# Gate and up projections in ten of eleven steps as seven block products instead of eight

## The reference

```python
D_FF = 2816
h2 = rms_norm_2(x, g_ffn[layer])
x = x + (jax.nn.silu(h2 @ w_ffn_gate[layer]) * (h2 @ w_ffn_up[layer])) @ w_ffn_down[layer]
return rms_norm_2(x, g_final)
```

## Time and profile before

| what | before |
|---|---|
| time, median of 3 runs | 1060.94 us (1060.84 to 1061.04) |
| span of the profiled execution | 1059.3 us |
| PE busy | 1049.7 us, 99% |
| PEld busy | 844.1 us, 80% |
| DVE busy | 509.0 us, 48% |
| ACT busy | 448.8 us, 42% |
| POOL busy | 400.2 us, 38% |
| mean granted PE clock | 0.999 of full speed |
| chain that ended last, by line | 1882 56%, 2194 23%, 1940 4%, 1971 3%, 2012 3% |

### The profile page before, as it was taken

The page is one execution under the profiler, slowest core; times in us unless marked ns, Lnnn a source line. Parts: engine busy times, 40 slices in busy tenths (PEclk is TensorE's granted clock), DMA queues, the critical chain, the costliest instruction groups (busy, mean ns, idle before and its releaser), DMA issues.

```text
span 1059.3 us, 14455 instructions
## 1 busy us (share of the span) xinstructions
PE 1049.7 (99%) x5545; PEld 844.1 (80%) x5545; DVE 509.0 (48%) x1061; ACT 448.8 (42%) x788; POOL 400.2 (38%) x300
## 2 busy tenths in 40 slices
PE   9999999999999999999999999999999999999997
PEld 8877897767678876888777888888888888888886
DVE  6766788875752316998587344230000000032444
ACT  6444457676653425233465414342221221233533
POOL 3455520001025333446000255434435354465772
PEclk9999999999999999999999999999999999999999
DMA  9541141201032331332221232223232323323221
GB/s 298 184 120 51 34 119 41 75 17 44 28 120 80 72 117 43 101 99 80 80 80 41 80 104 95 91 77 110 80 118 79 114 84 104 114 80 100 82 97 80
DMA packets 84724, 95.72 MB, mean 90 GB/s; under 512 B 8121, under 2 KB 70930, under 8 KB 84666
## 3 DMA queue, kind: packets, MB, share of 16 engines
q1 hardware_dynamic: 83706, 92.46, 28.0%
q0 software_dynamic: 560, 2.12, 0.6%
q10 hardware_dynamic: 400, 0.35, 0.1%
HBM read 92.80 MB, written 2.12 MB: 90 GB/s over the span
## 4 chain that ended last, share of the span: by engine, by line
PE 94%; DVE 4%; ACT 1%; issue 1%; POOL 0%; DVEq 0%; ACTq 0%; POOLq 0%
PE bank L1882 56%; PE bank L2194 23%; PE bank L1940 4%; PE bank L1971 3%; PE bank L2012 3%; PE bank L1988 1%; DVE L L1478 1%; PE bank L2169 1%; PE bank L1833 1%; PE bank L2098 1%; PE bank L2045 1%; DVE L L1524 1%; DVE pool L1483 0%; PE bank L2001 0%; PE bank L1964 0%
## 5 line engine op out<-in xcount | busy, mean ns | idle before, releaser
L1042 POOL TENSOR_TENSOR w_lo<-raw,w_hi 128x512 fp32r<-128x512 f32 (+1 forms) x190 | 267.2, 1436 | 415.7 <-ACT w_hi L1104 403.0
L1882 PE MATMUL bank<-h_hi,w_hi 128*128 128x512 f32 (+1 forms) x560 | 224.0, 400 | 0.3 <-ACT h_hi L1315 0.2
L1882 PE MATMUL bank<-h_hi,w_lo 128*128 128x512 f32 (+1 forms) x560 | 218.6, 390 | 0.0
L1882 PE MATMUL bank<-h_lo,w_hi 128*128 128x512 f32 (+1 forms) x560 | 217.8, 390 | 0.0
L1082 POOL TENSOR_TENSOR w_lo<-raw,w_hi 128x512 fp32r<-128x512 f32 x88 | 110.7, 1290 | 133.5 <-ACT w_hi L1353 67.1
L1104 ACT ACTIVATE w_hi<-raw 128x512 fp32r<-128x512 f32 (+3 forms) x94 | 111.2, 1213 | 116.1 <-PE bank L1882 113.8
L1882 PE MATMUL bank<-w_hi,h_hi 128*128 128x512 f32 (+2 forms) x397 | 145.3, 366 | 0.0
L1882 PE MATMUL bank<-w_lo,h_hi 128*128 128x512 f32 (+2 forms) x397 | 144.5, 364 | 0.0
L1882 PE MATMUL bank<-w_hi,h_lo 128*128 128x512 f32 (+2 forms) x397 | 144.5, 364 | 0.0
L2194 PE MATMUL bank<-h_hi,w_hi 128*128 128x512 f32 x352 | 137.1, 389 | 0.0
L2194 PE MATMUL bank<-h_hi,w_lo 128*128 128x512 f32 x352 | 137.0, 389 | 0.0
(11 more groups left out here) (213 smaller groups left out, 1260.3 us busy)
## 6 DMA issues: line engine op xcount, KB each, us to landing
raw<-in_w_in SPq DMA_DIRECT2D x29, 1024.0 KB, 5.3
raw<-in_w_ffn_gate SPq DMA_DIRECT2D x11, 1024.0 KB, 5.4
raw<-in_w_ffn_up SPq DMA_DIRECT2D x11, 1024.0 KB, 5.4
raw<-in_w_out SPq DMA_DIRECT2D x8, 1024.0 KB, 5.0
raw<-in_w_ffn_down SPq DMA_DIRECT2D x8, 1024.0 KB, 5.1
raw<-in_w_in SPq DMA_DIRECT2D x8, 512.0 KB, 4.6
pool<-in_cmp_w SPq DMA_DIRECT2D x4, 1024.0 KB, 9.1
raw<-in_w_ffn_down SPq DMA_DIRECT2D x4, 768.0 KB, 4.3
```

The lines of the kernel that those rows point to most:

```text
L1042: nc.gpsimd.tensor_tensor(w_lo[:, u.n % 2, cols], raw[:, u.n % 2, cols], w_hi[:, u.n % 2, cols].bitcast(F32), ALU.subtract).then_inc(lo_do ...
L1882: ins = mm(bank[t.bank][0:t.m, 0:u.width if u.token else T], stationary, moving, start=first and n == 0, stop=last and n == len(products) ...
```

## The change

Steps 1 to 10 of gate and up are computed in blocks. A unit's weight is cut into four blocks: k-tiles 0 to 3 or 4 to 7, output features 0 to 127 or 128 to 255. h is cut into four as well: the same halves of k, tokens 0 to 255 or 256 to 511. Eight block products (each 4 k-tiles x 3 = 12 matmuls of 256 columns) become seven by combinations of the blocks (the scheme of Strassen and Winograd): three plain weight blocks and four sums of weight blocks, three plain h blocks (used as they are) and four combinations of h (`t_hi`, `t_lo`), made once. The products of a unit run in the order b = 0 to 6; their banks are 0, 1, 2, 3, 0, 2, 3 of a set of four (banks 4 to 7 for j = 0, banks 0 to 3 for j = 1), the last three adding to what is in the bank. Step 0 (`ffn_first`) stays as it was.

For each unit, while the unit before is multiplied, DVE makes four weight sums (`weight_sum`, 128 x 512 out of `raw` into `L`), ACT makes seven high parts (`high_block`, 128 x 512, each into the place that product b of the unit before has just left), DVE the low parts of the four sums and POOL those of the three plain blocks. After the products ACT copies the first one (128 x 256) and DVE joins (`join`) the rest: u = P1 + P0, v = P2 + u, then the three other quarters of the output, 5 instructions of 128 x 256 a unit, and for j = 1 three gated products. Silu is applied to quarters, 4 instructions of 128 x 256 a step.

During step 0 DVE also makes h = hi + lo (`sum_parts`, two instructions of 128 x 2048), the four combinations (`comb`, 128 x 1024) and their low parts; ACT makes their high parts. SP loads now wait for the low parts of DVE (`lo_dve`) of the unit before in the same slot. The hand-over to down: ACT may split `act` once the first product of the last unit is done; the first down unit's weights are split in four pieces, each after one product of the last unit.

```diff
-    ffn_half = sem("ffn_half")
+    BLOCKS, SUMMED, PLAIN = 7, 4, 3
...
+        BLOCK_OF = (("w", 0, 0), ("s", 1), ("s", 2), ("s", 0), ("w", 0, 1), ("w", 1, 1), ("s", 3))
+        MOVING_OF = (("h", 0, 0), ("t", 1), ("t", 2), ("t", 0), ("h", 1, 0), ("t", 3), ("h", 1, 1))
+        SUM_BANK = (0, 1, 2, 3, 0, 2, 3)
...
@@ SyncE @@
+            with sp.Fori(2, FFN_STEPS) as f:
+                for j in range(2):
+                    sp.wait_ge(lo_dve, f * (2 * SUMMED) + (ffn_u[2 + j].lo_end - 4 * SUMMED))
+                    load_ffn(j, bass.ds(f * 256, 256))
...
@@ GpSimd @@
+                    def plain_lows(j, hi0):
+                        for b in (0, 4, 5):
+                            pool_e.wait_ge(hi_done, hi0 + b + 1)
+                            nc.gpsimd.tensor_tensor(ring_lo[b], block_source(n0 + j, b), ring_hi[b].bitcast(F32), ALU.subtract)\
+                                .then_inc(lo_plain, 1)
+                    ffn_lo(n0 + 1, order[n0 + 1].hi_end)
...
@@ ScalarE @@
+                        sc.wait_ge(prod_done, prod0 + 1)
+                        if j:
+                            sc.wait_ge(joined, join0 - 4)
+                        act_fn(first_term, unit_bank(j, 0), ACT.Copy).then_inc(first_copied, 1)
+                        for b in range(BLOCKS):
+                            ahead(b, prod0 + b + 1)
+                            if j == 0 and b == 4:
+                                sc.wait_ge(act_done, f * 3 + 2)
+                                sc.wait_ge(prod_done, prod0 + 5)
+                                silu_part(out_part(0, 0, 0), unit_bank(0, 4))
+                                sc.wait_ge(joined, join0 + 3)
+                                silu_part(out_part(0, 1, 1), out_part(0, 1, 1))
...
@@ VectorE @@
+                    def weight_sum(j, i, sums0, arrived, freed):
...
+                        x, y, op = ((w_block(n, 1, 0), w_block(n, 1, 1), ALU.add), (w_sums[0], w_block(n, 0, 0), ALU.subtract),
+                                    (w_block(n, 0, 0), w_block(n, 1, 0), ALU.subtract), (w_block(n, 0, 1), w_sums[1], ALU.subtract))[i]
+                        v.tensor_tensor(w_sums[i], x, y, op).then_inc(sum_done, 1)
...
+                        def join(out, b, other):
+                            v.tensor_tensor(out, unit_bank(j, b), other, ALU.add).then_inc(joined, 1)
+                        ve.wait_ge(prod_done, prod0 + 2)
+                        ve.wait_ge(first_copied, f * 2 + (j + 1))
+                        join(u_term, 1, first_term)
+                        ahead(0)
+                        ve.wait_ge(prod_done, prod0 + 3)
+                        ve.wait_ge(joined, join0 + 1)
+                        join(v_term, 2, u_term)
+                        ahead(1)
+                        ve.wait_ge(prod_done, prod0 + 4)
+                        ve.wait_ge(joined, join0 + 2)
+                        join(out_part(j, 1, 1), 3, v_term)
+                        ahead(2)
+                        if j:
+                            ve.wait_ge(prod_done, prod0 + 5)
+                            ve.wait_ge(gsilu, f * 4 + 6)
+                            v.tensor_tensor(act_part(f, 0, half_t[0]), unit_bank(1, 4), out_part(0, 0, 0), ALU.mult)\
+                                .then_inc(act_done, 1)
+                        ahead(3)
...
+                        def ahead(j, b, hi0, sums0, arrived, plain, freed):
+                            if b == 0:
+                                for i in range(4):
+                                    weight_sum(j, i, sums0, arrived, freed)
+                            low_block(j, b, hi0 + (b + 1), plain)
...
+                    sum_parts(0)
+                    comb(0, B[0][1], B[0][0], [(h_summed, 1)])
+                    sum_parts(1)
+                    comb(2, B[1][1], B[0][1], [(h_summed, 2)])
+                    comb(1, B[1][1], t1, [(comb_done, 1)])
+                    comb(3, B[1][0], t2, [(comb_done, 3)])
+                    for i in range(4):
+                        weight_sum(0, i, 0, ffn_u[2].arrived, None)
+                    for nth, i in ((1, 0), (2, 2), (3, 1)):
+                        comb_low(i, nth)
+                    for b in range(4):
+                        low_block(0, b, ffn_u[2].hi0 + b + 1, PLAIN)
+                    comb_low(3, 4)
+                    for j in range(2):
+                        gated(j)
...
@@ TensorE @@
+                        if b == 4:
+                            pe.wait_ge(first_copied, f * 2 + (j + 1))
+                        if b in (5, 6):
+                            pe.wait_ge(joined, s2 + (b - 3))
...
+                        if BLOCK_OF[b][0] == "w":
+                            pe.wait_ge(lo_plain, f * (2 * PLAIN) + (PLAIN * j + nth))
+                        else:
+                            pe.wait_ge(lo_dve, f * (2 * SUMMED) + (SUMMED * j + ffn_u[2].lo0 + nth))
+                        x_hi, x_lo = moving_parts(b)
+                        for k in range(4):
+                            for w, x in ((ring_hi[b], x_hi), (ring_hi[b], x_lo), (ring_lo[b], x_hi)):
+                                ins = mm(unit_bank(j, b), w[:, k, :], x[:, k, :], start=b < 4 and k == 0 and w is ring_hi[b] and x is x_hi,
+                                         stop=k == 3 and w is ring_lo[b], skip_group_check=True)
+                        ins.then_inc(prod_done, 1)
```

More of the change, by code:

```diff
@@ new lines, in _ @@
+                    silu_part(L[:, 0, :], bank[0][:, :])
+                    for i in (2, 1, 3):
+                        comb_high(i)
+                    sc.wait_ge(tile_done, t0 + 2)
+                    silu_part(L[:, 1, :], bank[1][:, :])
+                    for b in range(BLOCKS):
+                        high_block(0, b, ("tile_done", t0 + (2 if b < 4 else 4)), 0, ffn_u[2].arrived)
+                    step(0)
+                    with sc.Fori(1, FFN_STEPS - 2) as f:
+                        step(f)
@@ L1812, in _ @@
                 if kind == "ffn":
-                    t0 = e["tile"]
-                    def gated(f, j, x):
-                        ve.wait_ge(tile_done, f * 4 + (t0 + j + 3))
-                        ve.wait_ge(gsilu, f * 2 + (j + 1))
-                        v.tensor_tensor(x, bank[2 + j][:, :], L[:, j, :], ALU.mult).then_inc(act_done, 1)
-                    with ve.Fori(0, FFN_STEPS - 1) as f:
-                        for j in range(2):
-                            gated(f, j, pool[:, bass.ds(f * (2 * T) + T * j, T)])
@@ L1828, in _ @@
+                    step(0)
+                    with ve.Fori(1, FFN_STEPS - 2) as f:
+                        step(f)
+                    step(FFN_STEPS - 2, final=True)
         @block.tensor
@@ L2205, with step @@
+                    def step(f):
+                        for j in range(2):
+                            for b in range(BLOCKS):
+                                product(j, f, b)
+                    ffn_first()
+                    step(0)
+                    with pe.Fori(1, FFN_STEPS - 1) as f:
+                        step(f)
 _INS = ["x", "norm_g", "w_in", "diff_q_norm_g", "diff_k_norm_g", "diff_lambda_q1", "diff_lambda_k1",
```

242 lines of the change are left out of this document (189 added, 53 removed).

## The result

The changed kernel takes 1054.69 us (median of 4 runs, 1054.01 to 1055.0), the kernel before 1060.99 us (4 runs): a ratio of 0.9941, 95% interval 0.9929 to 0.9952. That is 6.3 us less; I had forecast 7.9 less, 1053.1 us. The profiled run is the fastest of the four: 1054.01 us, span 1052.1, 1.9 outside.

The account below looks back on a forecast made before the run. PE's matmuls were taken to bound the kernel. Saving 16.0 us, less 5.0 stop, 1.6 product 5, 0.6 handover and 1.0 clock, gives -7.8: span 1051.5, plus 1.6 outside, 1053.1 us; own range 1049 to 1057.

Parts of the forecast that it names:

- Matmuls: Gate and up, ten block steps: 168 matmuls of 0.120 us, 20.16 us a step against 21.76, saving 16.0 us.
- DVE in a step: Settled block step: DVE has 14.7 us of work plus 4 lost to POOL, 18.7 us, below PE's 20.16.
- The layout of one unit: One block unit laid out in time: first join starts 3.2 us, second join done 6.7, product 5 due 7.2.
- Rival (b): Block steps: POOL holds DVE off 1.29 us instead of 1.10, 22.4 us a step, 1073 us in all; chance 5%.
- The slack of 0.5 us: Each block unit: DVE's second join ends at 6.7 us, PE needs it at 7.2, so 0.5 us to spare.
- The stop in the first step: First step, PE's third tile waits for POOL's up-weight low parts, which take turns with DVE: 5.0 us lost.
- Product 5 of the first unit: First block unit: DVE, late in a row, ends the second join after product 5 is due: 1.6 us lost.
- The clock: Behind PE's stop in the first step, a stretch at the lower clock: between 0 and 2.3 us, taken as 1.0.
- The last unit: Handover to down: DVE makes low parts of `act` ahead of the gated product freeing bank 0; down starts 0.6 us late.
- Rival (a): Block steps: DVE and POOL set the pace, 21.3 to 21.9 us a step, 1063 to 1069 us; chance 25%.
- Rival (c): First step: POOL wins its turns, PE's stop is under 2 us, all hidden, 1046 to 1048 us; chance 12%.
- (d): Block steps: DVE late in some or PE's waits cost something, 0.3 to 1 us a step, 1056 to 1062 us; chance 13%.

Follow-up runs that it names:

- the run with DVE alone: Changed kernel, but DVE also makes the plain blocks' low parts and GpSimd does nothing inside the loop: 1053.66 us (one run).
- The run with one instruction more: Changed kernel plus one unread 128x256 DVE addition in each unit, between the first join and the weight sums: 1057.52 us (one run).
- the run by piece: Changed kernel, but in the first step PE waits for POOL's four low parts of the up weights one by one: 1053.49 us.
- a second old step: Changed kernel with two old steps and nine of block products, piecewise PE waits, and preparation and handover reordered: 1048.03 us; with DVE's first-unit work also reordered 1047.16.
- with two more: Changed kernel plus two unread 128x256 DVE additions in each unit, each ahead of a join: 1075.96 us (one run).
- with DVE alone and two more: Changed kernel with GpSimd idle inside the loop, DVE making all low parts, plus two unread DVE additions a unit ahead of joins: 1067.23 us (one run).
- the two versions without the stop: Changed kernel with two old steps, nine block steps and reordered preparation: 1048.03 us; the same with DVE's first-unit work in another order: 1047.16 us.

## Why the prediction was right, step by step

**Matmuls: right.** 0.120 us each, a step 20.16, in nine steps of ten without a break. The zero for the waits ahead of each product held: 1584 matmuls in one piece of the chain.

**DVE in a step: right.** Forecast 14.7 and about 4 of waiting for POOL, 18.7; the trace has 17.64 busy, and the run with DVE alone puts the waiting at 3.0. The layout of one unit was met within 0.1 us in every row shown. POOL's piece of 806.52 holds DVE off for 1.16 us from its start (the sum of 807.43 ends 808.36; less its own 0.68 that is 807.68), with 1.10 forecast and 1.29 as the rival's.
The Trainium skill, page "SBUF — State Buffer", section "Who interferes with whom", has the lock last for the whole instruction; in the trace DVE goes on at 1.16 of 1.29 us, so it doesn't bear this out to the end.

**Rival (b), the longer hold, was priced wrongly.** The 1073 us took all six pieces to be in the way at full length. With the layout's own two a unit, a hold of 1.29 makes about 14.7 + 4 x 1.29 = 19.9 us a step (an estimate), still under 20.16. The time of 1054.69 us therefore says nothing about the length of the hold; only the rows do.

**The slack of 0.5 us: too large.** The layout had the times right, but PE starts 0.12 us behind a join's end, so that 0.35 us were to spare. The run with one instruction more ends exactly there, and the next instruction already meets the other case.

**The stop in the first step: right.** 4.83 for 5.0, by the turns that I had laid out. What the prediction didn't see is that there was little to gain from PE's side: in the run by piece the stop comes back as 3.7 us at product 1.

**Product 5 of the first unit: the size right, the reason wrong.** 1.41 was measured for 1.6. The prediction gave "DVE late in a row" as the cause. But DVE stands idle for 2.57 us ahead of it, waiting for POOL's plain low parts, and with a second old step, where DVE is idle for 4.75 us before the unit and so isn't late at all, the wait is 1.32 us again. It hangs on the chain from the start of the unit by way of ACT and POOL to block 6's low part, which stands ahead of the sums in DVE's queue. That the number came out was luck.

**The clock: mis-sized.** 1.0 was taken between 0 and 2.3, 1.66 was measured in the profiled run. The 0.6 us by which the span passes the forecast (1052.1 for 1051.5) is about the size of this miss; the misses of the other terms and what lies outside them (-0.27 and +0.6) cancel to within 0.1. The cost isn't fixed either. The runs with one more, with two more and with DVE alone and two more have the same PE work up to there and the same stop, and lose 2.91, 2.49 and 2.80 us behind it; the run with DVE alone loses 1.70. So 1.66 is the low end, and the prediction's upper bound of 2.3 was too low. The mean clock is 0.996 in those three runs, and 0.995 in the other three of the changed kernel, which took 0.6 to 1.0 us more than the profiled one. That a longer stretch at the lower level is what they have too, up to 1.25 us more, is an inference, since they have no trace; it would be most of the rest of the difference between 1053.1 and 1054.69.
The Trainium skill, page "TensorE: Matmul & The Clock Gate", section "What's actually happening", lets the clock fall when PE idles, and both the changed kernel (after 4.67 us) and the run by piece (after 3.69) agree. In the run by piece the matmuls were 0.12 us apart for another 0.8 us before the lower level came. Stops of 0.7 to 1.5 us, as in each unit of the run with two more, left it at 1.00.

**The last unit: right, a little more.** 0.69 + 0.11 for 0.6.

**Outside the span:** 1.9 for 1.6.

**Rival (a), DVE and POOL set the pace:** it didn't happen, since DVE caught up within the first unit, as argued against it. The mechanism is real: two instructions of 0.33 us a unit are enough to reach it (ahead of the joins), one isn't (behind the first). The price was 21.3 to 21.9 us a step in the prediction and 22.5 in the run with two more, 1.3 us of which are the additions themselves. The sums nearly agree, but not their parts: the prediction had 6.6 us of holds and a DVE that never waits, the trace has 4.6 us of holds and 1.85 of waiting. The prediction also took five pieces in the way to be enough for this case; five hold something off in the changed kernel, for 0.25 to 1.10 us each, and its step is 20.16. Rival (c), all hidden, had POOL win its turns, which it didn't; (d) would have shown as steps above 20.16, and there are none but the first.

## What to carry to other kernels

Preparation that comes before a new form of the work needs cover for as long as it lasts: count it against the old work beside it, and if it doesn't fit, start the new form one step later. Here a block step given up cost 1.6 us, and with the order of the preparation changed as well the two versions without the stop came out 6.7 and 7.5 us below the changed kernel. Where two engines hold each other off, as DVE and POOL do here, an engine's share of busy time (88% of a step) says little on how near it is to setting the pace; add one or two small instructions to it and look where the step length leaves its floor.

## What the runs showed of the hardware

The lower clock also came after PE had stood for 3.7 us, not only after 4.7, and the matmuls of 512 columns then start 0.427 us apart, those of 256 columns 0.213 (0.227 and 0.120 otherwise). How long the lower level lasts differs from run to run: 1.66 to 2.91 us were lost behind one and the same stop. DVE's busy time in the profile holds the time in which POOL holds it off: it fell by 3 us a step in what it had been doing when POOL's six pieces a step were taken away. And help can cost more than it gives: for a DVE that runs late, POOL's six pieces saved it 3.6 us and cost it 4.6.
